# The channel mean behind the long convolution: GpSimd pre-adds three of the four tiles, TensorE sums two

## The reference, cut to what matters

```python
def conformer_conv(a, g, dw_w, dw_b, ln_g, ln_b):
    y = a * jax.nn.sigmoid(g)
    y = causal_depthwise_conv(y, dw_w, width=31) + dw_b
    return jax.nn.silu(layer_norm(y, ln_g, ln_b))      # mean and variance over 512 channels

def layer_norm(x, g, b):
    mu = mean(x, axis=-1); xc = x - mu
    return xc * rsqrt(mean(xc * xc, axis=-1) + EPS) * g + b
```

## Time and profile before

| | us |
|---|---|
| median of 3 runs (2349.87 to 2355.47) | 2350.24 |
| the profiled execution | 2350.0 |
| its span, first to last instruction | 2348.2 |
| PE busy | 2265.4 (96%) |
| DVE busy | 1121.8 (48%) |
| ACT busy | 938.4 (40%) |
| POOL busy | 677.1 (29%) |
| weight DMA (`wraw<-in_w_in_dram`), issue to landing, median | 3.8 |

### The profile page before, as it was taken

One profiled execution on the slowest core, in us unless ns is written; L12 is line 12 of the kernel. 1 busy time (PEld: TensorE's weight loads), 2 busy tenths in 40 slices (PEclk: granted clock), 3 DMA queues, 4 the chain that ended last, 5 costly groups with the idle time before them and its releaser, 6 DMA issues.

```text
span 2348.2 us, 26869 instructions
## 1 busy us (share of the span) xinstructions
PE 2265.4 (96%) x10928; PEld 1860.7 (79%) x10928; DVE 1121.8 (48%) x1621; ACT 938.4 (40%) x1365; POOL 677.1 (29%) x399
## 2 busy tenths in 40 slices
PE   7899999999999999999999999999989999999998
PEld 6688889886767787888887788778767778888876
DVE  5778664446435335444212879433443253332334
ACT  4756442234444335333322242435543343332334
POOL 1243323003112263232223222311232353332334
PEclk8999999999999999999999999999999999999999
DMA  8523111211122244433332522322211432333332
GB/s 286 153 81 108 46 37 55 63 41 51 53 59 75 73 144 130 134 108 117 95 99 76 152 90 83 97 81 72 81 55 54 144 90 81 108 93 96 105 98 94
DMA packets 347984, 220.65 MB, mean 94 GB/s; under 512 B 18394, under 2 KB 327245, under 8 KB 347861
## 3 DMA queue, kind: packets, MB, share of 16 engines
q1 hardware_dynamic: 338462, 202.31, 29.3%
q10 hardware_dynamic: 9398, 16.62, 2.1%
HBM read 210.49 MB, written 8.41 MB: 93 GB/s over the span
## 4 chain that ended last, share of the span: by engine, by line
PE 86%; DVE 6%; ACT 4%; issue 1%; POOL 1%; SPq 1%; DMA 0%; ACTq 0%; DVEq 0%; POOLq 0%
PE ps L343 84%; DVE arena L372 2%; ACT arena L361 1%; PE ps L346 1%; ACT scr L361 1%; DVE arena L364 1%; ACT whi L361 1%; DVE scr L372 1%; ACT L352 1%; SPq L3504 0%; POOL wlo L364 0%; ACT L361 0%; DVE arena L375 0%; POOL hlo L364 0%; DVE scr L364 0%
## 5 line engine op out<-in xcount | busy, mean ns | idle before, releaser
L364 POOL TENSOR_TENSOR wlo<-wraw,whi 128x1024 fp32r<-128x1024 f32 (+1 forms) x159 | 383.7, 2413 | 1098.7 <-ACT whi L361 1098.6
L361 ACT ACTIVATE whi<-wraw 128x1024 fp32r<-128x1024 f32 (+1 forms) x328 | 341.0, 1041 | 327.8 <-PE ps L343 275.0
L343 PE MATMUL ps<-hhi,whi 128*128 128x512 f32 x1664 | 445.6, 408 | 20.7 <-ACT hhi L361 8.9
L343 PE MATMUL ps<-hhi,wlo 128*128 128x512 f32 x1664 | 420.8, 392 | 3.5 <-POOL wlo L364 3.5
L343 PE MATMUL ps<-hlo,whi 128*128 128x512 f32 x1664 | 421.3, 392 | 1.8 <-POOL hlo L364 1.8
L343 PEld LDWEIGHTS ps<-hhi,whi 128*128 128x128 f32 x1664 | 313.3, 192 | 101.2 <-issue 26.7
L343 PEld LDWEIGHTS ps<-hlo,whi 128*128 128x128 f32 x1664 | 315.3, 190 | 70.6 <-POOL hlo L364 2.9
L343 PEld LDWEIGHTS ps<-hhi,wlo 128*128 128x128 f32 x1664 | 314.6, 189 | 70.4 <-POOL wlo L364 4.6
L364 DVE TENSOR_TENSOR wlo<-wraw,whi 128x1024 fp32r<-128x1024 f32 (+1 forms) x169 | 218.6, 1293 | 298.1 <-ACT whi L361 297.8
L343 PE MATMUL ps<-arena 128*128 128x128 f32 (+4 forms) x2272 | 310.0, 292 | 12.7 <-ACT arena L361 9.6
L343 PEld LDWEIGHTS ps<-arena 128*128 128x128 f32 x2272 | 274.7, 193 | 30.9 <-ACT arena L361 11.6
(11 more groups left out here) (201 smaller groups left out, 2560.4 us busy)
## 6 DMA issues: line engine op xcount, KB each, us to landing
wraw<-in_w_in_dram SPq DMA_DIRECT2D x99, 512.0 KB, 3.8
wraw<-in_w_ff_dram SPq DMA_DIRECT2D x64, 512.0 KB, 3.9
wraw<-in_ffn_w_up_dram SPq DMA_DIRECT2D x44, 512.0 KB, 3.8
wraw<-in_w_gate_dram SPq DMA_DIRECT2D x32, 512.0 KB, 3.5
arena<-in_w_ada_dram SPq DMA_DIRECT2D x20, 512.0 KB, 4.1
arena<-in_w_ada_dram SPq DMA_DIRECT2D x8, 1024.0 KB, 11.4
wraw<-in_ffn_w_down_dram SPq DMA_DIRECT2D x16, 512.0 KB, 3.6
wraw<-in_w_branch_dram SPq DMA_DIRECT2D x16, 512.0 KB, 3.4
```

The source lines that it names most:

```text
L343: return pe.e.matmul(o, l, r, start=start, stop=stop)
L361: return ac.e.activation(o, i, f, bias=bias, scale=scale, **kw)
L364: return q.e.tensor_tensor(o, a, b, op)
```

## The change

In step 14 POOL waits for tap 30 of tile 1 and writes `YD[0] + YD[1]` into `A[:, 50]` (signal `cva_po` 1). In step 21 it waits for tap 30 of tile 2 and adds `YD[2]` to it (`cva_po` 2). PE sums over the partitions of `A[:, 50]` and of `YD[3]` only. ACT waits until PE has read `A[:, 50]` before it writes the first square there.

```diff
@@ Tensor.conv
                 pe.wait_ge(*PA.free("cs"))
-                for m in range(4):
-                    pe.wait_ge(*at("cv_ve", m, 30))
-                    t = mm(bk[:, :], ones, YD[m], m == 0, m == 3)
-                t.then_inc(*inc("cv_mm", "s"))
+                pe.wait_ge(*at("cva_po", 2))
+                mm(bk[:, :], ones, A[:, 50, :], True, False)
+                pe.wait_ge(*at("cv_ve", 3, 30))
+                mm(bk[:, :], ones, YD[3], False, True).then_inc(*inc("cv_mm", "s"))
@@ Scalar.conv
                     ac.wait_ge(*at("cv_ve", "c", m))
+                    if m == 0:
+                        ac.wait_ge(*at("cv_mm", "s"))
@@ Gpsimd.conv
-                    for _ in range(7):
+                    for _ in range(6):
                         yield
+                    if m in (1, 2):
+                        po.wait_ge(*at("cv_ve", m, 30))
+                        if m == 1:
+                            for p in SG.ends("h3"):
+                                po.wait_ge(*p)
+                        else:
+                            po.wait_ge(*at("cva_po", 1))
+                        tt(po, A[:, 50, :], A[:, 50, :] if m == 2 else YD[0], YD[m], ALU.add).then_inc(*inc("cva_po", m))
+                    yield
```

## The result

The changed kernel is slower by 0.23%: ratio 1.0023 to the kernel before, 95% interval 1.0014 to 1.0032, 11 runs of each. The medians are 2358.55 and 2354.46 us, 4.1 us apart; the means, 2358.47 and 2353.05 us, are 5.4 us apart and give the ratio of 1.0023. A forecast of 2355.7 us against a median before of 2350.24 makes 1.0023 too, but with an interval of 0.09% (2.1 us) to either side that this agrees to the last digit is luck. The medians of both kernels lie above the forecast's base, since the first three runs of before had a median of 2350.24 and all eleven have 2354.46. Both kernels scatter by 6 to 7 us (before 2349.87 to 2355.88, changed 2354.74 to 2361.91).

A forecast was written before the change was run, and what follows sets the result against it. DVE's taps were taken to bound the kernel between 1444.06 and 1486.71, PE around that. Terms 2.7 + 2.0 + 0.8 = +5.5 us took 2350.0 to 2355.5; with the median 0.24 above, 2355.7 us, range 2350.5 to 2359.0.

The forecast's parts named there:

- PE's saving: At the mean: four of eight PE instructions go, worth 1.7 us, all ahead of a 2.02 us wait; gain 0.
- its condition: At the mean: PE's saving would begin to count if the last tap came more than 2.02 us earlier.
- First add: POOL's add in step 14 delays DVE about 1.1 us near 1408; covered, so cost 0, without the cover 1.1.
- First term: From 1446.12, step 22: second add and displaced av2 low part hold DVE's taps; +2.7 us (bounds 2.04 and 3.17).
- Second term: Ahead of the PSUM copies near 1474: POOL's low part overlaps late DVE taps; +2.0 us (bounds 0 and 2.85).
- Third term: At the mean: PE waits 7.2 us and its clock falls to 0.50 longer; +0.8 us (bounds 0 and 1.0).
- the long case: PE's clock at 0.50 from the first instruction after longer waits (1281.22, 1554.27) for 4.88 and 4.93 us: 2.45 lost.
- The sum: Whole kernel: 2.7 + 2.0 + 0.8 = +5.5 us, forecast 2355.7 us, +0.23%, called "the same" with 0.78.
- Rival 1: Only one POOL collision: gv6's low part still finds the PSUM copies; +3.5 us, 2353.7 us; chance 0.20.
- Rival 2: Not slower: displaced low part harmless, bias DMA's 1.45 us wait absorbs it; 2350.2 to 2351.0 us; chance 0.09.
- Rival 3: Slower by over 0.3%: one more PE half-rate stretch behind the convolution, 1.65 us; 2357.4 to 2358.9 us; chance 0.17.

The follow-up runs named there:

- 1: Kernel before with PE's part alone: two products at the mean (tiles 0 and 3), no adds on POOL; ratio 0.9995 (0.9986 to 1.0005).
- 2: Changed kernel with the four PE products of before, so only the two POOL adds are new; ratio to before 1.0024 (1.0014 to 1.0033).
- 3: Changed kernel with both adds one step later on POOL, the second behind the low part of av2; ratio to before 0.9996 (0.9987 to 1.0006).
- 5: Kernel before with the low parts of av6, gv2, gv6 and aq1 written by DVE instead of POOL; ratio 0.9981 (0.9971 to 0.9990).
- experiment 7: Kernel before with ACT's mark early, four low parts moved to DVE, and the change with its adds one step later; ratio 0.9974 (0.9964 to 0.9983).
- 8: Changed kernel with gv6's low part written by DVE instead of POOL; ratio to the kernel before 1.0009 (1.0000 to 1.0018).
- 4: Kernel before with the mark ACT waits for ahead of the four taps of step 22, not behind; ratio 0.9998 (0.9988 to 1.0008).
- 6: Kernel before with ACT's mark early and the low parts of av6, gv2, gv6 and aq1 on DVE; ratio 0.9983 (0.9974 to 0.9993).

## Why the prediction was right and where it was wrong

- **"Between 1444.06 and 1486.71 every microsecond that DVE's list loses is lost by the kernel."** Shown by 1, 2, 3 and 5: S moved by what DVE's taps lost or gained, until PE's wait was used up.
- **PE's saving, 0.** Shown by 1: 0.00 us of S, 1.72 us more wait. So is its condition: experiment 7 gains about 1.6 us with it once the wait is gone.
- **First add, 0.** Right in the changed kernel, where DVE waits 1.90 us for PE at the eviction, but with one more reason than I gave. The add cost the four taps beside it 0.89 us (6.04 for 5.15; 1.1 forecast), and 0.67 of them came back later, where eight taps meet POOL's next low part (7.60 us for 8.27). Before, and then the changed kernel:

```profile
1407.85 5.15 DVE L372 SCALAR_TENSOR_TENSOR arena<-arena,colv 128x512 f32<-128x512 f32 x4
...
1428.80 8.27 DVE L372 SCALAR_TENSOR_TENSOR arena<-arena,colv 128x512 f32<-128x512 f32 x8
...
1411.45 6.04 DVE L372 SCALAR_TENSOR_TENSOR arena<-arena,colv 128x512 f32<-128x512 f32 x4
...
1433.40 7.60 DVE L372 SCALAR_TENSOR_TENSOR arena<-arena,colv 128x512 f32<-128x512 f32 x8
```

So even in experiment 3, where the second low part isn't displaced and nothing is offset by that, DVE comes to the eviction only some hundredths of a microsecond behind PE, and "without the cover 1.1" was too much.
- **First term, +2.7 us.** Measured 2.93 on the taps, 0.92 for the add (0.7 forecast) and 2.01 for the low part (2.04). The add took 1.53 us and not 1.39, and it began 0.17 us after the TENSOR_SCALAR of tile 3, beside which I took it to run freely. The TENSOR_SCALAR lost nothing (0.54 us as before); whether the add was held by it, the trace doesn't tell. PE's stop at av4 was 1.23 us (1.2 expected).
- **Second term, +2.0 us.** Measured 2.02, and shown to be the low part of gv6 by 8. The two terms make 4.95; S grew by 4.85, since DVE's own low part behind the copies took 1.21 us for the 1.31 of before.
- **Third term, the clock, +0.8 us: wrong.** This is the term of the sum that was mis-sized. The last products at 1495.17 and all behind them lost no more than before: the piece of the chain behind is 55.23 us for 55.40, so the term is -0.2, outside its bounds of 0 and 1.0. I had reckoned that behind a long wait the clock is down for 4.9 us of work. Windows of PE in the changed kernel (columns as in the earlier trace rows):

```profile
1488.10:1491.50 3.40, 0.00 (x1) 0.97 0.40 96
1491.50:1495.10 3.60, 0.00 (x0) 0.50 0.07 11
1495.10:1498.40 3.30, 3.23 (x6) 0.54 1.10 293
1498.50:1502.00 3.50, 3.50 (x17) 1.00 0.03 6
```

The clock fell to 0.50 at about 1491.3, while PE stood, and was back at 1498.1. What lay in the wait, 3.9 us, cost nothing, and 2.9 us of work at half rate cost 1.5. In the two rows from which I took the long case the clock had also fallen in the wait, but later, 1.8 and 1.7 us ahead of the work:

```profile
1279.40:1281.20 1.80, 0.00 (x0) 0.51 0.00 0
...
1552.50:1554.20 1.70, 0.00 (x0) 0.50 0.00 0
```

In the other runs the loss at the mean, half of the work that was done at 0.50, was 1.7 us behind waits of 2.02 (before), 2.03 (4), 3.74 (1) and 4.75 (3), 1.5 behind 5.35 (2), 1.9 behind 6.05 (8) and 1.5 behind 7.06. So the length of the wait doesn't set the price; what sets it is how much of the time at 0.50 falls on work. Why the clock falls early in one wait and late in another stays open.

- **The sum and what was made of it.** 5.5 us were forecast; 4.67 are measured from the eviction to the DMA out of `ext_dram`, and the means of the runs differ by 5.4. The step that failed is the one behind the sum: "A measurement of this kernel can tell about 0.3% (7 us) from no change, so by that measure this is 'the same'", with 0.78 on it. With 11 runs of each the interval was 0.09% (2.1 us) to either side, and 0.14% to 0.32% is slower. The mechanism had been worked out to +5.5 us, with no term under nothing, and then was given away to a limit of 7 us for which no row was shown; three runs that scatter by 5.6 us don't say what eleven can tell. It should have been called slower, however small.
- **Rival 1** (one collision) didn't happen in the changed kernel; experiment 8 made it, with one collision of 2.9 us left, and experiment 3 left the smaller one of 0.9. **Rival 2** (not slower) fell with the first term: the wait for the bias DMA moved along, 1.55 us long in both kernels. **Rival 3** (one more stretch at half rate behind the convolution) didn't come. At the wait of 3.95 us that it names the profiled execution went the other way: before, PE worked at 0.50 from 1554.27 on for 4.93 us; now it started at 1562.41 and was at 0.50 for some 3.4 us, which gives back about 0.8 us.

```profile
1563.00:1566.40 3.40, 3.40 (x9) 0.50 0.54 154
```

## What to carry to other kernels

Before work is taken from an engine, look at what stands between it and the next wait in the chain: work ahead of a wait is free already, and taking it away is worth something only after the wait is gone. An operation put on an idle engine is priced by how long it holds up the engine on the chain, and by what is queued behind its wait: here the displaced low part cost twice what the add did. When a change moves one engine against another by a few microseconds, look for the next meeting of the two: covers that were there by accident are lost in either direction. And when the sum of a forecast has a sign, say it, before asking what a measurement can resolve.

## What the runs showed of the hardware

**POOL holds DVE.** Beside a low part of POOL (2.4 us) DVE's taps lose 2.0 us, beside an add of 1.5 us 0.9 us; DVE's own low part behind the copies took 2.83 us for 1.31 (experiment 4). DVE's eight copies from PSUM took 2.73 or 2.74 us in all ten traces, with POOL beside them (before, 1, 3, 4) or without. The same low part written by DVE itself costs 1.14 us. So beside DVE's taps the low part on POOL was dearer for DVE than doing it.

**Part of the scatter of the times is the clock's.** Whether the granted clock of PE goes down at a given stop of PE differs between traces with the same instructions up to there. Behind the stop of 2.67 us ahead of 684 it stayed up in the traces of before and of experiments 3, 4, 5 and 8, and went down in those of the changed kernel and of 1, 2, 6 and 7. Before:

```profile
686.00:690.00 4.00, 4.00 (x19) 1.00 0.00 0
```

The changed kernel, whose instructions are the same there:

```profile
686.00:690.00 4.00, 4.00 (x13) 0.60 0.00 0
```

Behind the stop of 2.3 us ahead of 1297 it went down in the traces of the changed kernel and of experiments 1, 2, 4, 6 and 7, and not in those of before, 3, 5 and 8. Before, and then the changed kernel, which does the same work 2 us later:

```profile
1298.20:1301.60 3.40, 3.40 (x17) 1.00 1.02 306
...
1300.20:1303.60 3.40, 3.40 (x10) 0.50 1.01 303
```

PE's starts in the two traces show what this cost. The changed kernel's trace is 0.44 us behind that of before at 684, 1.99 at 1281, 1.98 at 1297 and 3.61 at 1390.90. So the two places cost 1.55 and 1.63 us and make most of the 3.61 us that this execution had lost before it reached the change. A few such places fit the spread of 6 us in the runs of one kernel; that all of the spread comes from them is not shown.
